# Three key pages a job in the gate stage, none in the second gate, and early page slots for the output projection

## The reference

```
layer 0 (GLA):  proj = rms_norm(h) @ gla_w_in ; q, k, v, g, gk from it
                o = gla_chunked(q, k, v, gk)       # chunks of 64 tokens, state carried from chunk to chunk
                h = h + (rms_norm(o) * silu(g)) @ gla_w_out
                h = h + sigmoid(rms_norm(h) @ w_ple_gate[0]) * (p[0] @ w_ple_up[0])
k, v = rms_norm(h) @ w_kv                          # shared by the layers that follow
layer 1 (stick-breaking attention): q, g = rms_norm(h) @ sb_w_in
                z = q.k / sqrt(64) + bias ; A[t,s] = sigmoid(z_ts) * prod_{s<j<t} (1 - sigmoid(z_tj))
                h = h + (A v * silu(g)) @ sb_w_out ; then ple_add as in layer 0
y = rms_norm(h)
```

## Time and profile before

| | |
|---|---|
| median of three runs | 909.92 us |
| the profiled execution's own time | 909.13 us |
| its span | 907.1 us |
| PE busy | 867.3 us (96%) |
| DVE busy | 564.5 us (62%) |
| POOL busy | 279.1 us (31%) |
| mean DMA rate | 256 GB/s |

### The profile page before, as it was taken

How to read it: one execution, slowest core, us unless ns; L and a number is a source line. 1 busy time by engine, 2 the same in 40 slices (tenths; PEclk the granted TensorE clock), 3 DMA queues, 4 the chain that set the end, 5 groups by cost and what they waited for, 6 DMA issues and landing times.

```text
span 907.1 us, 14970 instructions
## 1 busy us (share of the span) xinstructions
PE 867.3 (96%) x5141; PEld 605.6 (67%) x5141; DVE 564.5 (62%) x680; ACT 451.0 (50%) x1521; POOL 279.1 (31%) x148
## 2 busy tenths in 40 slices
PE   5999999999999999999998999999989999999995
PEld 3556677877764444444477887787755544899994
DVE  4545385787957768997999642222267777553553
ACT  4601392323476667768864522122178676434433
POOL 3000001954428998996766000000100000021110
PEclk9989999999999999999999999999999999999998
DMA  9798978652469987988999159998898879321202
GB/s 331 261 373 302 373 255 283 212 194 76 151 208 389 393 318 250 362 314 307 375 350 308 48 194 332 340 325 320 302 325 294 316 271 359 109 93 48 93 1 95
DMA packets 109307, 232.49 MB, mean 256 GB/s; under 512 B 7409, under 2 KB 66424, under 8 KB 109232
## 3 DMA queue, kind: packets, MB, share of 16 engines
q1 hardware_dynamic: 50736, 171.64, 52.0%
q10 hardware_dynamic: 58496, 59.90, 19.8%
HBM read 220.38 MB, written 11.14 MB: 255 GB/s over the span
## 4 chain that ended last, share of the span: by engine, by line
PE 70%; DVE 11%; ACT 8%; DMA 6%; issue 3%; POOL 1%; SPq 1%; ACTq 0%; DVEq 0%; POOLq 0%
PE pp L1562 19%; PE pp L1565 12%; PE pp L1549 11%; PE pp L1969 6%; PE pp L1926 4%; DMA s<-in_state_gla_dram 3%; PE pp L1526 2%; DVE slot L1246 2%; PE pp L1953 2%; DMA slot<-in_cache_k_dram 2%; ACT slot L796 2%; PE pp L1940 2%; PE pp L1577 2%; PE pp L1642 1%; POOL slot L602 1%
## 5 line engine op out<-in xcount | busy, mean ns | idle before, releaser
L602 POOL TENSOR_TENSOR slot<-slot,qb 128x1024 f32<-128x1024 f32 x94 | 248.3, 2668 | 122.7 <-DMA slot<-in_cache_k_dram 69.4
L796 ACT ACTIVATE slot<-slot 128x64 f32<-128x64 f32 x480 | 114.8, 241 | 31.1 <-POOL slot L602 31.1
L1247 DVE TENSOR_REDUCE zall<-slot 128x16 f32<-128x1024 f32 x98 | 118.1, 1214 | 10.6 <-POOL slot L602 9.4
L1070 DVE TENSOR_TENSOR w_lo<-w_raw,w_hi 128x1024 fp32r<-128x1024 f32 x57 | 75.3, 1322 | 71.5 <-ACT w_hi L654 71.4
L654 ACT CAST w_hi<-w_raw 128x1024 fp32r<-128x1024 f32 x58 | 60.5, 1045 | 69.3 <-PE pp L1565 21.5
L796 ACT ACTIVATION_READ_ACCUMULATOR slot<-slot 128x1 f32 x480 | 90.0, 188 | 0.0
L1549 PE MATMUL pp<-xn,w_raw 128*128 128x512 f32 x192 | 84.4, 593 | 0.2 <-ACT xn L665 0.2
L1549 PE MATMUL pp<-xn,w_unsplit 128*128 128x512 f32 x192 | 83.9, 592 | 0.0
L1565 PE MATMUL pp<-xa_hi,w_hi 128*128 128x512 f32 x200 | 82.5, 413 | 0.0
L1565 PE MATMUL pp<-xa_hi,w_lo 128*128 128x512 f32 x200 | 79.9, 400 | 0.0
L1565 PE MATMUL pp<-xa_lo,w_hi 128*128 128x512 f32 x200 | 79.7, 399 | 0.0
(11 more groups left out here) (302 smaller groups left out, 1509.6 us busy)
## 6 DMA issues: line engine op xcount, KB each, us to landing
slot<-in_cache_k_dram SPq DMA_DIRECT2D x128, 512.0 KB, 6.2
slot<-in_cache_v_dram SPq DMA_DIRECT2D x120, 512.0 KB, 5.4
w_raw<-in_gla_w_in_dram ACTq DMA_DIRECT2D x12, 1024.0 KB, 6.8
slot<-in_gla_w_in_dram SPq DMA_DIRECT2D x24, 512.0 KB, 11.1
w_raw<-in_w_kv_dram ACTq DMA_DIRECT2D x8, 1024.0 KB, 10.6
w_raw<-in_w_ple_gate_dram ACTq DMA_DIRECT2D x6, 1024.0 KB, 5.1
s<-in_state_gla_dram SPq DMA_DIRECT2D x1, 4096.0 KB, 27.5
out_dram<-s ACTq DMA_DIRECT2D x4, 1024.0 KB, 8.5
```

Of the source, the lines that this page charges most:

```text
L602: nc.gpsimd.tensor_tensor(slot[s][:], slot[s][:], qb[:, (n // NPG) % 2, :], ALU.mult).then_inc(S("k_mul_pool"), 1)
L796: ins = nc.scalar.activation(part, part, ACT.Copy, accum_out=zall[:, n % NPG, b * SH + h:b * SH + h + 1])
L1070: nc.vector.tensor_tensor(lo, raw, hi.bitcast(F32), ALU.subtract).then_inc(S("w_split"), 1)
L1247: nc.vector.tensor_reduce(zall[:, n % NPG, b * SH:(b + 1) * SH], at.rearrange("p (h d) -> p h d", d=HD), AX.X, ALU.add).then_inc(S("k_used ...
```

## The change

Three things change together.

- The page counts: each job of g takes 3 pages instead of 2, and g1 takes none. With 8 pages in v, 24 in g and 32 each in wo0, ple0 and q1 all 128 are placed. `FEW` becomes 32.
- The slots: pages from `FEW` on go round slots 0 to 7 beginning with 0. The wait for the last head, and the load of `w_up0` behind it, move to page `FEW` + 4, which is the first one in slot 4.
- POOL no longer waits for the gated heads before wo0's pages.

```diff
 PAGES_AT = {}
-for _name, _c in (("v", (0, 0, 0, 0, 2, 2, 2, 2)), ("g", (2,) * 8), ("wo0", (4,) * 8), ("ple0", (4,) * 8),
-                  ("q1", (4,) * 8), ("g1", (4, 4, 0, 0, 0, 0, 0, 0))):
+for _name, _c in (("v", (0, 0, 0, 0, 2, 2, 2, 2)), ("g", (3,) * 8), ("wo0", (4,) * 8), ("ple0", (4,) * 8),
+                  ("q1", (4,) * 8)):
...
-SLOT_OF += [n % 4 if n < FEW else (4, 5, 6, 7, 0, 1, 2, 3)[(n - FEW) % 8] for n in range(NPAGES)]
+SLOT_OF += [n % 4 if n < FEW else (n - FEW) % 8 for n in range(NPAGES)]
...
-                if n == FEW:
+                if n == FEW + 4:
 
                     sp.wait_ge(S("o_mm"), GH)
                     sp.wait_ge(S("st_out"), 16 * GH)
...
             for j in range(PHASES["v"][0], PHASES["K"][0]):
-                if j == PHASES["wo0"][0]:
-                    pool.wait_ge(S("gated"), GH)
                 multiply_pages(j)
```

## The result

| | before | after |
|---|---|---|
| median | 909.02 us (906.46 to 911.26, 4 runs) | 933.67 us (931.39 to 936.06, 4 runs) |
| span of the profiled execution | 907.1 us | 933.0 us |
| PE busy | 867.3 us | 877.0 us |

The ratio is 1.0273, with a 95% interval of 1.0243 to 1.0303: the change makes the kernel 24.6 us slower. The sign was forecast; 918.5 us and the range of 911 to 925 were not enough.

A forecast was written before the change was run, and what follows sets the result against it. PE was taken as the bound, busy 867.3 of 907.1 us. Terms 2.5 + 3.2 + 4.0 + 1.7 - 2.4 = 9.0 us on 909.13 gave 918.1, predicted as 918.5 against the median, range 911 to 925.

The forecast's parts named there:

- part 1: In g, DVE's added third-page sums delay PE in the fourth, fifth/sixth and eighth jobs: 2.5 us.
- part 2: At the third and fourth heads' gating, DVE instructions slowed beside POOL's products, one and a half meetings: 3.2 us.
- part 3: In wo0, page 36 lands late behind SP's in-order queue, so PE waits for ACT's third-tile square: 4.0 us.
- part 4: Half clock on PE behind the long wait in wo0, charged once: 1.7 us, bounds 0 and 3.4.
- part 5: In g1, without its key pages, PE's two waits for `evac` go: 2.4 us gained.
- everything in full: Rival over gate and wo0: four meetings, 7.1 us in wo0, the clock twice, 928.1 us; chance 0.08.

The follow-up runs named there:

- filled: Changed kernel with idle matmuls on PE ahead of its five long waits: 925.18 us, ratio 1.0182.
- no_pool_wait: Kernel before without POOL's wait for the gated heads, nothing else changed: 914.10 us, ratio 1.0075.
- one_early: Changed kernel with POOL's wait restored, only page 32 going early and pages for slots 4 to 7 right behind it: 922.69 us, ratio 1.0163.
- slots_alone: Kernel before with only the new slots and SP's later wait and w_up0 load; page counts and POOL's wait as before: 914.35 us, ratio 1.0063.
- tuned: Kernel before with nine idle matmuls at its 2.2 us wait, a third page in g's eighth job alone, g1 at 4 and 3: 909.81 us, 1.0028.
- even_third: Kernel before with a third page in g's second, fourth, sixth and eighth job, four pages in g1: 910.42 us, ratio 1.0025.
- counts_alone: Kernel before with only the new page counts, three in every job of g and none in g1: 924.56 us, ratio 1.0154.
- odd_third: Kernel before with a third page in g's first, third, fifth and seventh job, four pages in g1: 919.76 us, ratio 1.0152.
- short_sum: Kernel before with only the new page counts, DVE's sum of each gate job's third page cut to one of 16 heads: 917.97 us, 1.0117.

## Why the prediction was right or wrong

Most places and mechanisms were right, and most sizes too small. In the change's own trace:

| term | forecast | measured | from |
|---|---|---|---|
| part 1, third sums | 2.5 | 3.4 | three times 1.13 |
| part 2, meetings | 3.2 | 7.3 | 1.60 twice, 2.02, 2.13 |
| part 3, wait for the square | 4.0 | 5.7 | PE's wait |
| end of ple0 | 0 | 1.8 | PE's wait |
| part 4, clock | 1.7 | 8.7 | four windows |
| part 5, g1 | -2.4 | -3.3 | PE, 29.3 us behind to 26.0 |
| sum | 9.0 | 23.6 | span 25.9 |

Of the other 2.3 us 1.2 lie ahead of the gate, where the two kernels are the same, 0.4 at the wait for the first head's states, and 0.7 at the new wait for `q1T`. Matmul by matmul, PE was 28.6 us behind the trace of before when g1 began, 29.3 behind that wait, and 26.0 when g1 ended. Parts 1 and 2 are DVE's delays, 10.7 us; PE's three waits for them add up to 10.2.

- **Part 4 is the step that failed most:** "the wait of 4 us in wo0 is longer, so I add 1.7 once; bounds 0 and, with a second such wait at the gating, 3.4". I charged the clock once and for one length, while my own parts 1 and 2 named three more places with waits; I had kept each apart and so under the size of the earlier trace rows. Added up at one place (a sum and a meeting on the same chain) each reaches 2.5 us. And behind the waits of 5.2 and 5.7 us the half clock lasted 6.8 us, not 3.5. `filled` shows the clock by itself, 8.3 us with the fifth wait in it. The page "TensorE: Matmul & The Clock Gate" of the Trainium skill, whose rule I cited (section "HAM oscillation — how this bites in real kernels"), says of a kernel that waits for DMA that it is paid again at each wait. The change's trace agrees at all four, though they are waits for another engine's result, and I hadn't carried it into the sum; in other versions some such waits go free (last section).
- **Part 2** took one and a half meetings at the end of the gate alone. There were two at the third head, and I had left out the fourth and sixth job, where one more came each. My own figure of 7.2 us of products in 11 us a job was the warning. I had it also that the fourth head's gating might meet POOL; it didn't, because POOL's pages for wo0 were late. That case is `no_pool_wait`.
- **Part 1** was right in its rule and nearly in its size; the sixth job had no more slack than the fourth (1.13, not 0.3).
- **Part 3** was right in mechanism (`one_early`), and short by 1.7 us in size. In the change, page 36 landed 13.8 us after page 33's issue (297.77, landed 311.58) where I had 12.0. The DMA engines were full in that stretch (1.05, at 387 GB/s); what went to SP's queue of it was less, 3.15 MB in 13.8 us or 0.23 MB/us, where the earlier trace rows gave 0.28. In `slots_alone` the wait was 4.2 us and the clock 1.2, close to the forecast's 4.0 and 1.7, but for other pages and with g1 giving back 2.9, so that is no test of the size. The lag that came to the end of ple0 I hadn't seen.
- **Part 5** came out in number, and the net gain (28.6 to 26.0) is 2.6. But its working was wrong: I gave each wait to the pages next to it. `tuned` and `even_third` take pages from g1's second job and gain nothing, and `slots_alone` leaves all eight pages in g1 and loses both waits. So the gain isn't shown to come from g1 having no pages; what makes DVE late or not there stays open.
- **The rivals:** everything in full, 928.1, was nearest; it had four meetings, 7.1 us in wo0 and the clock twice. I gave it 0.08, since "a later PE gives POOL time to finish before the last gating". That was true of the last head only. That it came so near was in part luck: its meetings were 1.1 us too many, and its clock was 5.3 us too little. The range ended at 925 because its terms were priced each for itself, and the clock, which hangs on all of them, only once.

## What to carry to other kernels

Price a wait of PE with the clock behind it, and add up first everything that lies on the same chain: a sum of 1.1 us and a meeting of 1.6 together made a wait of 2.5 us, and with the clock behind it PE lost 4.1. Ahead of an instruction that PE waits for, look at what else runs at that time on the engine that can slow it, and put extra work into the jobs that have no such instruction (1.0025 against 1.0152 for the same four pages). In a queue that is in order, what waits for something late should stand behind what could already go (`one_early`, 9.8 us). And a wait that looks idle may keep two engines apart (`no_pool_wait`, 5.7 us).

## What the runs showed of the hardware

- The half clock doesn't follow from a wait's length alone. A wait of 2.50 us was followed by 3.4 us at 0.54 in the change (229.22), and one of 2.50 us in `counts_alone` and one of 2.42 us in `odd_third` by none. In one trace, that of `short_sum`, a wait of 2.09 us was followed by half clock and one of 2.18 us by full. The windows behind these two, and behind the 2.42 us of `odd_third`:

```profile
228.40:231.80 3.40, 3.35 (x8) 2.61 (x9) 2.97 (x4) 2.70 (x3) 0.00 (x0) 0.54 0.41 109
254.40:257.80 3.40, 3.40 (x15) 2.77 (x16) 3.40 (x5) 2.76 (x4) 0.00 (x0) 1.00 0.27 82
```

```profile
226.40:229.80 3.40, 3.40 (x15) 2.78 (x16) 2.77 (x3) 2.77 (x3) 0.00 (x0) 1.00 0.45 117
```

  A sum that charges each such wait can so be off by 1.6 us a wait either way.
- It differs between executions of one kernel too. In the ten of `no_pool_wait` the mean granted clock is 0.991 in the fastest (910.51 us) and 0.980 in the slowest (921.78 us). A clock term read from one trace need not be that of the median.
- Matmuls that compute nothing, put where PE would wait, kept the clock at 1.00 and gave back 8.3 us of 24.6 (some 5 either way): here the clock was lost to standing still.
- A DVE instruction on two SBUF inputs on a POOL product of 2.4 us took mostly 2.07 to 2.89 us instead of 0.68. DVE's sums of one input took the same time beside them: two in 2.34 us at 242.89 in the change, while POOL multiplied from 237.50 to 246.93.
